# Conversions of a weight tile into its low part on GpSimd, each issued as two operations of half the columns

## What is computed

```python
def block(x, cond, lp, ctx=None):
    sh1, sc1, gt1, sh2, sc2, gt2 = ada_mod(cond, w_ada, b_ada)
    h = rmsnorm(x, g_mix) * (1 + sc1) + sh1
    gq, gk, gv, gr, zf, zb, nq, nk, nv, m_gla, m_na = split_in(h @ w_in)
    ...
    o_gla, s_f, s_b = gla_bidir(q, k, v, la_f, la_b, s0_f, s0_b)
    b_gla = (rmsnorm(o_gla, g_gla).reshape(B, T, GLA_V) * jax.nn.silu(gr)) @ w_gla_o
    ...
    b_na = o_na.reshape(B, T, NA_W) @ w_na_o
    mix = (jax.nn.sigmoid(m_gla) * b_gla + jax.nn.sigmoid(m_na) * b_na) @ w_out
    x = x + gt1 * mix
    h2 = rmsnorm(x, g_ffn) * (1 + sc2) + sh2
    x = x + gt2 * conv_ffn(h2, w_up, w_conv, b_conv, w_down)
```

## Time and profile before

| | us |
|---|---|
| median of 3 runs | 1088.03 (1086.72 to 1089.21) |
| the profiled execution | 1087.97 |
| its span, first to last instruction | 1086.2 |
| PE busy | 1028.5 (95%) |
| POOL busy | 483.4 (45%) |
| DVE busy | 588.3 (54%) |
| ACT busy | 434.6 (40%) |
| the 73 conversions of line 453 on POOL | 192.8, mean 2643 ns |
| mean granted TensorE clock | 0.984 |

### The profile page before, as it was taken

How to read it: one execution, slowest core, us unless ns; L and a number is a source line. 1 busy time by engine, 2 the same in 40 slices (tenths; PEclk the granted TensorE clock), 3 DMA queues, 4 the chain that set the end, 5 groups by cost and what they waited for, 6 DMA issues and landing times.

```text
span 1086.2 us, 19005 instructions
## 1 busy us (share of the span) xinstructions
PE 1028.5 (95%) x7419; PEld 944.7 (87%) x7419; DVE 588.3 (54%) x1059; ACT 434.6 (40%) x675; POOL 483.4 (45%) x296
## 2 busy tenths in 40 slices
PE   4899999899899999999999978999999999999998
PEld 4789999898698888999988878999999999688886
DVE  5524039994566563233253797777777777731102
ACT  3242252332656664222231454555545555521110
POOL 2164631351522131232244146788887876333331
PEclk9889999999999999999999988999999999999999
DMA  9766222112100112746634112222233321222231
GB/s 353 242 78 98 72 64 59 40 40 59 49 19 23 40 40 79 245 153 210 207 129 166 39 40 79 78 79 78 79 87 98 88 79 40 78 78 75 72 115 68
DMA packets 126603, 103.64 MB, mean 95 GB/s; under 512 B 5790, under 2 KB 102851, under 8 KB 126531
## 3 DMA queue, kind: packets, MB, share of 16 engines
q1 hardware_dynamic: 121568, 95.11, 28.6%
q0 software_dynamic: 1504, 3.15, 2.1%
q10 hardware_dynamic: 3459, 4.40, 1.2%
HBM read 98.18 MB, written 3.41 MB: 94 GB/s over the span
## 4 chain that ended last, share of the span: by engine, by line
PE 59%; POOL 18%; DVE 12%; issue 3%; ACT 3%; DVEq 0%; POOLq 0%; ACTq 0%
PE PJ L588 9%; POOL behind L550 8%; PE PJ L589 8%; PE PJ L593 8%; POOL ahead L550 5%; PE PA L956 3%; PE PA L958 3%; PE PA L957 3%; PE PJ L956 3%; PE PJ L958 3%; PE PJ L957 3%; POOL behind_val L558 2%; POOL ahead_val L558 2%; PE PA L894 2%; DVE A L1771 2%
## 5 line engine op out<-in xcount | busy, mean ns | idle before, releaser
L453 POOL TENSOR_TENSOR wlo<-wraw,whi 128x1024 fp32r<-128x1024 f32 x73 | 192.8, 2643 | 362.4 <-ACT whi L1132 266.2
L588 PE MATMUL PJ<-h_hi,whi 128*128 128x320 f32 x640 | 199.1, 319 | 5.8 <-DVE h_lo L1647 5.0
L589 PE MATMUL PJ<-h_lo,whi 128*128 128x320 f32 x640 | 195.7, 314 | 0.0
L593 PE MATMUL PJ<-h_hi,wlo 128*128 128x320 f32 x640 | 148.1, 313 | 0.0
L588 PEld LDWEIGHTS PJ<-h_hi,whi 128*128 128x128 f32 x640 | 122.9, 192 | 8.7 <-issue 6.7
L1132 ACT ACTIVATE whi<-wraw 128x1024 fp32r<-128x1024 f32 x52 | 54.8, 1055 | 174.5 <-PE PJ L593 92.1
L589 PEld LDWEIGHTS PJ<-h_lo,whi 128*128 128x128 f32 x640 | 122.9, 192 | 0.0
L593 PEld LDWEIGHTS PJ<-h_hi,wlo 128*128 128x128 f32 x640 | 109.4, 192 | 0.0
L1490 ACT ACTIVATE whi<-wraw 128x1024 fp32r<-128x1024 f32 x21 | 22.2, 1059 | 110.0 <-PE PJ L958 56.6
L2052 DVE SCALAR_TENSOR_TENSOR PJ<-u_all,vec,PJ 128x641 f32<-128x641 f32 x44 | 39.2, 890 | 48.7 <-ACT PJ L1448 48.7
L1076 PE MATMUL PA<-h_hi,behind 128*128 128x320 f32 x192 | 59.3, 309 | 0.0
(11 more groups left out here) (425 smaller groups left out, 2858.7 us busy)
## 6 DMA issues: line engine op xcount, KB each, us to landing
wraw<-in_w_in_dram SPq DMA_DIRECT2D x82, 256.0 KB, 3.1
ada_rest<-in_w_ada_dram SPq DMA_DIRECT2D x32, 512.0 KB, 5.6
wraw<-in_w_up_dram SPq DMA_DIRECT2D x48, 256.0 KB, 3.3
wraw<-in_w_down_dram SPq DMA_DIRECT2D x44, 256.0 KB, 2.8
raw_even<-in_w_up_dram SPq DMA_DIRECT2D x40, 256.0 KB, 3.7
ada_lo_half<-in_w_ada_dram SPq DMA_DIRECT2D x4, 1024.0 KB, 9.6
ada_hi_half<-in_w_ada_dram SPq DMA_DIRECT2D x4, 1024.0 KB, 15.5
wraw<-in_w_out_dram SPq DMA_DIRECT2D x16, 256.0 KB, 3.2
```

Source lines behind the costliest of these rows:

```text
L453: pool.tensor_tensor(wlo[:, slot, 0:k, :], wraw[:, slot, 0:k, :], whi[:, slot, 0:k, :].bitcast(F32), ALU.subtract).then_inc(lo_done, 1)
L588: pe.matmul(out, whi[:, slot, w0 + k, :], hi(k)[:, tok], start=start and k == k0, stop=False)
L589: pe.matmul(out, whi[:, slot, w0 + k, :], lo(k)[:, tok], start=False, stop=False)
L593: mm = pe.matmul(out, wlo[:, slot, w0 + k, :], hi(k)[:, tok], start=False, stop=stop and k == k1 - 1)
```

## The change

Each call of `lo` issues two subtractions instead of one: columns blocks 0 to 3 of the tile, then 4 to 7. The wait stands before the first, and `lo_done` is counted up by the second alone, so every waiter still waits for the whole tile. Nothing else changes.

```diff
             def lo(slot, ready, k=8):
 
                 pool.wait_ge(hi_done, ready)
-                pool.tensor_tensor(wlo[:, slot, 0:k, :], wraw[:, slot, 0:k, :],
-                                   whi[:, slot, 0:k, :].bitcast(F32), ALU.subtract).then_inc(lo_done, 1)
+                for part in (slice(0, k // 2), slice(k // 2, k)):
+                    ins = pool.tensor_tensor(wlo[:, slot, part, :], wraw[:, slot, part, :],
+                                             whi[:, slot, part, :].bitcast(F32), ALU.subtract)
+                ins.then_inc(lo_done, 1)
```

## The result

The changed kernel takes 1090.38 us (median of 22 runs, 1087.15 to 1096.73); the kernel before, timed beside it, 1087.58 (22 runs, 1085.34 to 1091.18). The ratio is 1.0025, with a 95% interval of 1.0013 to 1.0037: 2.7 us slower (1.4 to 4.0). That lies inside the predicted range, 0.3 above the predicted 1090.1. Part of this nearness is luck: the forecast was a rise of 2.1 us, and it was added to a start value, the profiled 1087.97, that is 0.4 above the median of the 22 runs.

What follows compares the result with a forecast made beforehand. PE, busy 95% of the span, was taken as the bound. 1087.97 + 0.3 (own cost) + 0 + 0 + 1.8 (passage) gave 1090.1 us; the forecast case spanned 1089.2 to 1091.8, the range 1086.2 to 1091.8.

Steps and rivals of the forecast that it cites:

- The passage, +1.8: Into the output projection: POOL's next low part goes between the two `row_diag`, delaying PE's second spread matmul by 1.8 us.
- two ends for the clock: At the passage: +0.9 us if the new wait lies inside the same slow stretch, +3.5 if it brings a second.
- The own cost, +0.3: Two operations per conversion take 0.2 us longer; PE waits for a low part near 100.73 us: +0.3, bounds 0.1 to 0.6.
- the turns: Where POOL and DVE collide, they alternate operation by operation, so a second half follows the first waiting DVE instruction.
- The levels, 0: GLA levels: the second subtraction ends at 213.00 instead of 213.03; no change, bounds -0.1 and +0.1 us per five collisions.
- Queries and keys, 0: Scaling of queries and keys: the fourth operation ends within 0.1 us of before, so no change.
- signs of being wrong: Second subtraction in a level taking 0.8 us, `mix_lo` still taking 1.9, or the clock's slow stretches lying elsewhere.
- The second tile of the down projection, 0: DVE's gain is POOL's loss; PE starts at 931.52 against 931.49: 0, bounds -0.1 and +0.2 us.
- Even exchange: At the passage, the second half precedes `mix_lo` or the second `row_diag` precedes POOL; only +0.3 stands, 1088.3 us; chance 0.22.
- Not separate: POOL keeps the port between halves; some ten places on PE's path lose 0.1 to 0.2 us each: 1089.5; chance 0.10.
- Faster: In GLA levels, second halves run during DVE's copies out of PSUM: 1086.8 us, or 1085.1 with the clock; chance 0.16.
- Starved: Second tile of the down projection: a second half waits for six more DVE low parts; 1094.4 us; chance 0.10.

Runs made afterwards that it cites:

- Passage alone: The kernel before with only the one conversion at the passage into the output projection in halves; median 1090.16 us, ratio 1.0021.
- ACT held: The changed kernel, with ACT waiting for the second `row_diag` before its first high part of `out_w`; median 1087.96 us, ratio 1.0001.
- attention start alone: The kernel before with only the two conversions beside the scaling of queries and keys, ahead of the attention, in halves; median 1087.76 us, ratio 1.0005.
- Quarters: The changed kernel with conversions in four pieces of 256 columns, except the one at the passage, which is whole; median 1090.57 us, ratio 1.0023.
- all but the passage: The changed kernel with the one conversion at the passage into the output projection whole again; median 1087.34 us, ratio 1.0005.
- second half held: The kernel before with the passage's conversion in halves, the second waiting until both `row_diag` are done; median 1090.69 us, ratio 1.0016.

## Why the prediction came out

**The passage, +1.8: the right place and the right mechanism, the size a bit low.** Every step of it is in the trace of after: `mix_lo` between the halves and 0.8 us long; ACT's `out_w` at once behind the table load; POOL's turn between the two `row_diag` (3.44 us for both, where I had put 3.5); an idle time of PE before the second spread. Passage alone shows that this one conversion is enough, ACT held that the turn is the cause. I had named two ends for the clock, 0.9 and 3.5. Measured from the output projection to the end it is 2.3 to 2.4 us, with 1.43 more of waiting, and the low clock twice as long. The passage itself takes 2.65 more (44.38 against 41.73), of which 1.2 come back by 680 us; another 0.9 lie behind that, where the kernels with a whole conversion differ by 1.2 among themselves; attention start alone has 0.8 there with its passage as before. So 1.4 to 1.5 us are shown to be the passage's in the traces, and the rest of the 2.3 is not.

**The own cost, +0.3: right as a wait, too small as a list.** PE's wait for the low part went from 0.76 to 1.06 us, and a cut costs 0.17 to 0.2. But I looked only at the place where PE waited already for a low part, and called all others covered. The 0.27 us in the attention are this same cost: I had put `rin_wide` at 0 by the turns, and there, at two places, the first of the two is held 0.13 us longer by the longer conversion.

**The levels, 0: the step that failed.** The turns came as predicted, and four of the five collisions cost PE nothing (within 0.1 us). The fifth, at the end of the levels, did: I worked out that DVE is held up no longer, and forgot that POOL now is, by one more DVE operation (6.49 us instead of 5.07), and PE needs that low part. I had also worked out a level with four subtractions of 640 columns and taken it for all; the last two collisions stand beside one subtraction and one copy of 1280 columns (L1754 to L1759), so the operation that goes between the halves is longer there. The levels lost 0.57 us, beyond my bounds of 0.1 for each collision.

**Queries and keys, 0: nearly.** 0.24 us were gained, because DVE waits for ACT in between and part of POOL's work falls into that pause, which the sum of turns left out. Behind this place the changed kernel's trace has a slow stretch that the trace before lacks; stretches that lie elsewhere were one of my signs of being wrong. It isn't seen in the median of this change alone, and it is no proof against the turns, since a kernel with whole conversions there shows it too.

**The second tile of the down projection, 0: right.** PE waits 1.66 us against 1.73, now for POOL. Quarters show that this was near an edge: there the same place costs 1.35 us of waiting and a fall of the clock.

**The sum.** 1.0 for all but the passage and 2.3 for the passage is 3.3, against 2.7 (1.4 to 4.0) timed. My 2.1 was low by the levels, the attention and what lies behind the passage. That the time came out 0.3 from the forecast, with pieces that add up to 1.2 more than mine, is partly luck.

**The rivals.** Even exchange is out: POOL took the turn in both traces with halves at the passage and nothing held. Not separate is out: each half waited for its own DVE operation. Faster is out in the levels, where it was meant: PE's waits there were 6.4 us with wholes, halves and quarters. Its idea, a piece that finds a gap, came true only ahead of the attention, for 0.24 us. Starved is out as the cause. The one conversion that was starved before still is, and at a place where PE has slack (next section).

## What to carry to other kernels

Where two engines hold each other up and take turns, cutting one engine's operation in two doesn't shorten what a row of the other's operations loses, as long as that row outlasts the cut operation, and it ends the cut operation later by one operation of the other engine for each further piece, with all that waits for its end. It does help where the row is short and its engine then waits for a third one (here 0.24 us with halves and 0.76 with quarters). What helps is to move the whole operation to where the other engine works out of PSUM, if the consumer and the next load into its buffer can wait that long. And an operation that ends earlier can free a third engine (here ACT) whose follow-up takes the port at a worse moment, so the follow-up wants a wait of its own.

## What the runs showed of the hardware that I had not expected

Small operations of DVE are held like large ones: 16 columns took 1.13 us at the passage (L1943), as long as half a conversion, and 0.17 in the kernel with the second half held.

Turns are not kept everywhere. In the changed kernel, as in the earlier trace rows, a conversion that asks in the middle of a running row of `prod_lo` gets the port only when the row is over; with quarters, in the same row, it gets it after one operation. The two timelines, changed kernel first:

```profile
963.52 5.22 DVE L2144 TENSOR_TENSOR prod_lo<-prod,act_late 128x640 fp32r<-128x640 f32 x7
966.26 4.89 POOL L454 TENSOR_TENSOR wlo<-wraw,whi 128x512 fp32r<-128x512 f32 x2 [5.55 <-ACT whi L1492]
```

```profile
958.17 6.87 DVE L2145 TENSOR_TENSOR prod_lo<-prod,act_late 128x640 fp32r<-128x640 f32 x7
960.82 4.82 POOL L455 TENSOR_TENSOR wlo<-wraw,whi 128x256 fp32r<-128x256 f32 x4 [4.72 <-ACT whi L1493]
```

In the first DVE runs its seven at 0.735 us each and POOL's two halves end 4.89 us after the request, in the second both alternate. What decides between the two isn't settled. The Trainium skill ("SBUF — State Buffer", section "Who interferes with whom") says that whoever issues first has the shared ports for the whole instruction and the other blocks; the held subtractions and quarters above agree with that. None of these runs shows what decides between a row of operations that runs on and one that yields after each.
